# A hybrid decoder block on one core: gate, logit and projection jobs in a new order, one moving block for identity and router, residual added in a late expert

## The chip, the cores and the metric

One Trainium2 chip, one core of it. The metric is the device time of one launch in microseconds, the median of several runs. TensorE (PE in the profile) multiplies matrices into PSUM, its weight loads stand apart as PEld; VectorE is DVE, ScalarE is ACT, GpSimd is POOL. SyncE (SP) here issues transfers (DMA) and computes nothing. Each engine runs its own list of instructions in order and waits on semaphores.

## The reference

One layer with 256 tokens (T) of 1024 numbers, all in fp32: a mixer with two branches and then 32 experts.

```python
xn = rms_norm(x, norm1_g)
proj = xn @ w_in
u, q, k, v, qi, ki, wi, gs, ga = jnp.split(proj, IN_OFFSETS, axis=-1)
...
y_ssm = s5_mixer(u, ssm_parameters)         # diagonal complex scan over the tokens, gelu, GLU
y_att = dsa_attention(q, k, v, qi, ki, wi)  # indexer scores choose 64 keys a query, then softmax
mixed = g_ssm * (y_ssm @ w_proj_ssm) + g_att * (y_att @ w_proj_attn)
x = x + mixed @ w_out
x = x + moe(rms_norm(x, norm2_g), expert_weights)  # 4 of 32 experts a token, clamped SwiGLU
...
return rms_norm(x, norm_f_g)
```

The experts' weights are 32 times 12.6 MB and all are read.

## The kernel before

**Layout.** In the mixer features lie on the 128 partitions and tokens along the free axis. The weights of the mixer come as 27 chunks of 1 MB (CHUNKS) through four buffers (wbuf, NBUF = 4): SP loads a chunk once the job that used its buffer last is done. TensorE works them off as jobs (JOBS): a job (feature_job, L974) is 16 matmuls of 128 x 128 weights and 256 tokens into one of two PSUM banks (rot), which ScalarE or VectorE must empty before the job after next. The profile counts two instructions for each fp32 matmul, so 32 for a job. JOBS and CHUNKS fix positions that the semaphores count to, so the order in the lists and in each engine's program is written out by hand and must agree.

**Scan.** U0 and U1 give u. VectorE builds the table phase by doublings (doubled, 1 to 64), ScalarE (turned) and VectorE (finish_phase, L636) make its second half. In four rounds (round_) TensorE makes input products (bu, L1005), VectorE multiplies them by the phase, adds, scans (L689) and makes the output products (out_ok), and TensorE turns those into y (y_out, L1016). After round 3 the ropes rotate keys, indexer queries and queries, y_raw adds the skip (L728), ScalarE takes the gelu (L482) and GLU0 and GLU1 follow.

**Attention.** Score jobs (score_job, L1068) are laced into A0 and A1; ScalarE takes the relu, VectorE adds up 16 heads (scores, L744), chooses keys with MAX8 and MATCH_REPLACE8 (choose_keys), masks the logits (mask, L769 and L772; row_max), ScalarE takes exponentials (L470), VectorE divides (probabilities; prob_ok). TensorE turns them (L1097) and multiplies by v (attend, L1105). PS0 to PS3 project the scan's branch, L1138 the attention's; W0 to W7 (L1161) make the mixer's output, added to x1.

**Into the experts.** After each W job aux (L1149, L1150) turns the tile of x1 to token rows: a matmul against w_rout (router logits, 32 columns) and one against the identity (128 columns). The identity products stay in banks 4 to 7, where they serve three ends: the squares for the second norm (L502), the tokens' rows xs (L510), and as the residual, as all experts add into the same banks (scatter, L1203). VectorE then picks four experts a token (L816 to L837) and each expert's one-hot tile; TensorE gathers the rows (L1186), turns them (L1194), multiplies by the expert's input weights (L1227; biases L1238) and output weights (L1269).

**Transfers.** The experts' weights come in 12 parts of 2,097 KB for two experts at a time (load_first(n) loads part n; even experts use 0 to 5, odd 6 to 11). The first 12 go into room that the mixer has left, when it has left it; part 5 covers the room of gate_s. Later ones follow chunk_used, part by part.

## Time and profile before

| | |
|---|---|
| median of 3 runs | 1187.84 us (1187.19 to 1189.55) |
| profiled execution | 1187.95 us, its span 1186.1 us |
| mean granted clock of TensorE | 0.987 of 2.4 GHz |
| busy: PE, PEld, DVE, ACT, POOL | 1121.3, 493.6, 343.7, 152.6, 0.7 us |
| first expert matmul | 275.41 us from the start |
| moved by DMA | 436.49 MB, mean 368 GB/s |

The span runs from the first to the last instruction. All times in rows count from its start. A row of a timeline merges neighbouring instructions of one group: start, length, engine, line, what it writes and reads, how many, and in brackets how long the engine was idle before and who ended that. The busy share of an engine is an average over stages that have different limits; a stage has to be read by itself.

### The profile page before, as it was taken

How to read it: one execution, taken by the hardware profiler on the slowest of the kernel's cores; microseconds unless marked ns; L12 is line 12 of the kernel's file. 1: busy time of each engine (PE TensorE's matmuls, PEld its weight loads, DVE VectorE, ACT ScalarE, POOL GpSimd, SP SyncE). 2: the span in 40 equal slices, each digit the busy share in tenths (PEclk: the TensorE clock that was granted, in tenths of full speed). 3: DMA queues.
4: the chain of work that ended last, by engine and by line, in shares of the span. 5: the costliest groups of instructions: out<-in, count | busy, mean ns of one | idle time of the engine just before them, and what ended most of it. 6: DMA issues, size and time to landing. Idle time of an engine off the chain costs nothing.

```text
span 1186.1 us, 13814 instructions
## 1 busy us (share of the span) xinstructions
PE 1121.3 (95%) x5602; PEld 493.6 (42%) x5602; DVE 343.7 (29%) x745; ACT 152.6 (13%) x317; POOL 0.7 (0%) x7
## 2 busy tenths in 40 slices
PE   8989988988999999999999999999999999999995
PEld 6868776873333333333333333333333333333331
DVE  7999656312111111112221111111111111111112
ACT  2301234112001000001100100000000000000002
POOL 0000000000000000000000000000000000000000
PEclk9999998998999999999999999999999999999998
DMA  8224715857999999999999999999999999999993
GB/s 333 107 107 143 319 72 220 347 195 298 427 429 426 430 427 430 427 429 428 429 428 429 429 428 429 428 428 427 430 427 430 427 430 427 429 428 429 427 428 156
DMA packets 33290, 436.49 MB, mean 368 GB/s; under 512 B 3824, under 2 KB 4080, under 8 KB 5232
## 3 DMA queue, kind: packets, MB, share of 16 engines
q1 hardware_dynamic: 32976, 435.43, 87.5%
q10 hardware_dynamic: 288, 0.69, 0.2%
q8 instruction: 19, 0.31, 0.1%
q14 instruction: 7, 0.06, 0.0%
HBM read 435.06 MB, written 1.05 MB: 368 GB/s over the span
## 4 chain that ended last, share of the span: by engine, by line
PE 73%; DMA 13%; DVE 6%; SPq 4%; ACT 2%; issue 1%; another core or an unknown queue 0%; DVEq 0%
PE ps L1227 30%; PE ps L1269 15%; DMA mem<-in_w_moe 12%; PE ps L974 8%; PE ps L1186 4%; PE ps L1203 4%; DVE mem L559 4%; SPq L351 4%; PE ps L1161 2%; PE ps L1238 2%; PE ps L1194 1%; PE ps L1254 1%; PE ps L1138 1%; DVE mem L689 1%; PE ps L1068 1%
## 5 line engine op out<-in xcount | busy, mean ns | idle before, releaser
L1227 PE MATMUL ps<-mem,late 128*64 128x512 f32 x2048 | 458.2, 595 | 22.8 <-DMA mem<-in_w_moe 22.6
L1227 PEld LDWEIGHTS ps<-mem,late 128*64 128x64 f32 x2048 | 141.6, 137 | 330.7 <-issue 282.3
L1269 PE MATMUL ps<-mem,late 128*64 128x512 f32 x1024 | 226.8, 595 | 0.0
L902 DVE TENSOR_SCALAR late<-ps 128x512 f32<-128x512 f32 x32 | 22.1, 692 | 689.4 <-PE ps L1227 689.4
L974 PE MATMUL ps<-mem 128*128 128x256 f32 x640 | 148.3, 391 | 8.0 <-ACT mem L482 3.7
L974 PEld LDWEIGHTS ps<-mem 128*128 128x128 f32 x640 | 123.6, 196 | 31.0 <-issue 11.3
L1269 PEld LDWEIGHTS ps<-mem,late 128*64 128x64 f32 x1024 | 70.7, 137 | 133.3 <-issue 128.1
L522 ACT ACTIVATE late<-late 128x512 f32<-128x512 f32 x32 | 20.1, 630 | 514.8 <-DVE late L902 514.8
L1186 PE MATMUL ps<-xs,late 128*64 128x512 f32 x256 | 63.7, 619 | 1.1 <-ACT xs L510 1.1
L1203 PE MATMUL ps<-late 64*128 64x512 f32 x256 | 63.6, 615 | 0.8 <-ACT late L529 0.8
L559 DVE TENSOR_TENSOR mem<-mem 128x1024 f32<-128x1024 f32 (+7 forms) x83 | 60.5, 770 | 8.3 <-ACT mem L421 7.1
L529 ACT ACTIVATE late<-ps 128x512 f32<-128x512 f32 x32 | 19.1, 597 | 230.7 <-PE ps L1269 230.7
L559 DVE TENSOR_TENSOR late<-late 128x128 f32<-128x128 f32 (+2 forms) x98 | 38.4, 419 | 5.9 <-ACT late L513 0.3
L1203 PEld LDWEIGHTS ps<-late 64*128 64x128 f32 x256 | 22.1, 186 | 41.8 <-issue 41.8
L1238 PE MATMUL ps<-bias_rows,late 32*64 32x512 f32 x256 | 34.8, 613 | 0.0
L1186 PEld LDWEIGHTS ps<-xs,late 128*64 128x64 f32 x256 | 15.9, 138 | 43.4 <-issue 42.3
L559 DVE TENSOR_TENSOR late<-ps,vec 128x512 f32<-128x512 f32 x32 | 22.1, 692 | 38.8 <-PE ps L1194 38.8
L518 ACT ACTIVATE late<-ps 128x512 f32<-128x512 f32 x32 | 19.2, 599 | 76.9 <-PE ps L1186 76.9
L1161 PE MATMUL ps<-mem 128*128 128x256 f32 x128 | 28.8, 379 | 0.0
L559 DVE TENSOR_TENSOR mem<-ps,mem 128x1024 f32<-128x1024 f32 (+2 forms) x26 | 23.2, 932 | 11.3 <-PE ps L1138 11.1
L1161 PEld LDWEIGHTS ps<-mem 128*128 128x128 f32 x128 | 23.9, 190 | 3.0
L1254 PEld LDWEIGHTS ps<-table,late 128*128 128x128 f32 x128 | 13.4, 140 | 28.1 <-issue 24.3
(157 smaller groups left out, 515.2 us busy)
## 6 DMA issues: line engine op xcount, KB each, us to landing
mem<-in_w_moe SPq DMA_DIRECT2D x192, 2048.0 KB, 42.3
mem<-in_w_mix SPq DMA_DIRECT2D x27, 1024.0 KB, 5.8
out<-xs SPq DMA_DIRECT2D x2, 512.0 KB, 3.1
late<-in_mix_tables SPq DMA_DIRECT2D x1, 576.0 KB, 15.2
mem<-in_x_t ACTq DMA_DIRECT2D x1, 512.0 KB, 4.5
mem<-in_x_t SPq DMA_DIRECT2D x1, 512.0 KB, 5.8
mem<-in_b_blk SPq DMA_DIRECT2D x1, 512.0 KB, 10.5
mem<-in_c_blk SPq DMA_DIRECT2D x1, 512.0 KB, 16.0
```

The source lines that it names most:

```text
L351: sp.dma_start(place_of(half, n), expert_part(e, n)).then_inc(moe_in[half][n], 16)
L522: ac.activation(sig, gate_z, ACT.Sigmoid, scale=ALPHA).then_inc(sig_ok, 1)
L559: return ve.tensor_tensor(out_, a, b, op)
L902: ve.tensor_scalar(gate_z, z[:, 0], LIMIT, None, ALU.min).then_inc(z_gate, 1)
L974: i = pe.matmul(b[:, m * T:m * T + T], slot[:, k, (first_m + m) * P:(first_m + m + 1) * P], src[:, k, :], start=(k == 0), stop=(k == kt - 1))
L1161: i = pe.matmul(b[:, 0:T], wide(f"W{m // 2}")[:, k, (m % 2) * P:(m % 2) * P + P], mixed[:, k, :], start=(k == 0), stop=(k == KD - 1))
L1186: i = pe.matmul(ps[64 * q:64 * q + SLOTS, 3, :], one_hot[:, t, :], xs[:, t, 512 * q:512 * q + 512], start=(t == 0), stop=(t == TT - 1))
L1203: i = pe.matmul(ps[:, 4 + 2 * t + q, :], gated_t[r, t * P:t * P + P], y_tok[r, :], start=False, stop=False, skip_group_check=True)
L1227: i = pe.matmul(ps[r, n // 2, :], h_sel[:, k % 4, k // 4, :], w[:, 512 * n:512 * n + 512], start=(k == 0), stop=(k == KD - 1))
L1238: pe.matmul(ps[r, n // 2, :], chosen[g, n, :], b_in[g, :], start=False, stop=False)
L1254: i = pe.transpose(ps[:, 0, n * P:n * P + P], act[:, n * P:n * P + P], ident)
L1269: i = pe.matmul(ps[64 * q:64 * q + SLOTS, 2, :], act_tile(k), w[:, 512 * q:512 * q + 512], start=(k == 0), stop=(k == KF - 1))
```

## The change

It changes orders and a few operations, and the result is computed as before.

- U0's chunk is loaded in two halves, laid out so that the first half serves the first eight matmuls; the mean matmul goes between the halves. The square sums go ahead of the doublings, the doubling by 64 is split, and the first quarter releases ScalarE.
- finish_phase of the next round moves in front of the output products. The ropes of keys and indexer queries go ahead of round 3, that of the queries behind it with its own temporaries.
- TensorE's order: input and output products move a job later or earlier; score jobs are laced into S3 and A0; y_out(3) behind them; A1, A2 and logits(0) ahead of GLU; A3 and logits(1), PS0, PS1 between them and the turning of probabilities; attend(0) behind PS2 and PS3.
- scores takes the two token tiles in turn. VectorE evicts PS2 and PS3 itself and multiplies by the gate in two steps.
- aux is one matmul of 160 columns a tile against turn_w, identity and router columns side by side; its result is evicted (rpart, xs), the router's parts are added up by VectorE (rsum), x is scaled in place.
- The residual is added in the last expert but one by four matmuls with diag, the identity times the root, on the normed xs. The second expert's scatter opens the banks.
- Parts 5 and others are loaded at other points of SP's list. The title of the change also names GpSimd; its three memsets are not touched by the diff.

The diff, cut to its core:

```diff
...
-JOBS = ["U0", "U1", "KK", "QI0", "QI1", "QI2", "QI3", "VW", "Q0", "Q1", "S0", "S1", "S2", "S3", "KR0", "KR1", "KR2",
-        "A0", "A1", "GLU0", "GLU1", "A2", "A3", "P0_0", "P0_1", "PS0", "PS1", "PS2", "PS3"] \
+JOBS = ["U0", "U1", "KK", "QI0", "QI1", "QI2", "QI3", "VW", "Q0", "Q1", "S0", "S1", "S2", "KR0", "KR1", "KR2", "S3",
+        "A0", "A1", "A2", "GLU0", "GLU1", "A3", "PS0", "PS1", "P0_0", "P0_1", "PS2", "PS3"] \
...
-CHUNKS = ["U0", "U1", "KK", "QI0", "QI1", "QI2", "QI3", "VW", "Q0", "Q1", "S0", "S1", "S2", "S3", "A0", "A1", "GLU",
-          "A2", "A3", "PS0", "PS1", "PA0", "PA1", "W0", "W1", "W2", "W3"]
+CHUNKS = ["U0", "U1", "KK", "QI0", "QI1", "QI2", "QI3", "VW", "Q0", "Q1", "S0", "S1", "S2", "S3", "A0", "A1", "A2",
+          "GLU", "A3", "PS0", "PS1", "PA0", "PA1", "W0", "W1", "W2", "W3"]
...
-            load("U0")
+            sp.dma_start(wbuf[:, 0, 0:1024], io["w_mix"][0, :, 0:1024]).then_inc(u0_first, 16)
+            sp.dma_start(wbuf[:, 0, 1024:SW], io["w_mix"][0, :, 1024:SW]).then_inc(w_slot_in[0], 16)
...
-            sp.wait_ge(scanned, 4)
             sp.wait_ge(out_ok, 4)
             load_first(0, 1)
+            load("GLU")
             sp.wait_ge(y_raw_ok, 1)
             load_first(4)
-            for name in CHUNKS[CHUNK["A2"]:CHUNK["PA0"]]:
+            for name in CHUNKS[CHUNK["A3"]:CHUNK["PA0"]]:
                 load(name)
+            sp.wait_ge(row_max, 1)
+            sp.dma_start(turn_w, io["turn_w"].rearrange("p (k c) -> p k c", k=KD)).then_inc(rout_in, 16)
             sp.wait_ge(y_ssm_ok, 1)
             load_first(2)
+            load("PA0")
+            load("PA1")
             sp.wait_ge(row_max, 2)
             load_first(6)
-            for name in CHUNKS[CHUNK["PA0"]:CHUNK["W2"]]:
-                load(name)
-            sp.wait_ge(gate_s_used, 1)
-            load_first(5)
+            load("W0")
+            load("W1")
             sp.wait_ge(att_done, 2)
             load_first(7)
...
             sp.wait_ge(aux_done, KD)
             load_first(11)
+            sp.wait_ge(rstd_ok, 1)
+            load_first(5)
...
-                ac.wait_ge(half_ok, 1)
+                ac.wait_ge(half_ok, min(i, 1) + 1)
...
+            gate("S", gate_s, V_BG, 3)
+            ac.wait_ge(roped, 3)
+            relus(3, 4, 5, 6)
             gate("A", gate_a, V_BG + KD, 0)
-            ac.wait_ge(roped, 4)
-            relus(3, 4, 5, 6)
-            gate("A", gate_a, V_BG + KD, 1)
...
+            gate("A", gate_a, V_BG + KD, 1)
+            gate("A", gate_a, V_BG + KD, 2)
...
-            gate("A", gate_a, V_BG + KD, 2)
+            exponentials(0)
             gate("A", gate_a, V_BG + KD, 3)
-            exponentials(0)
+            for n in range(2):
+                evict(f"PS{n}", p_ssm[:, 2 * n:2 * n + 2, :], pair)
+            prob_turned(0)
+            exponentials(1)
             attended(0)
-            exponentials(1)
-            for n in range(4):
-                evict(f"PS{n}", p_ssm[:, 2 * n:2 * n + 2, :], pair)
+            prob_turned(1)
             attended(1)
...
+                b = ps[:, 2 + m % 2, 0:TT * (P + NE)].rearrange("p (t c) -> p t c", t=TT)
                 ac.wait_ge(aux_done, m + 1)
+                ac.activation(rpart[:, m], b[:, :, P:P + NE], ACT.Copy).then_inc(rpart_ok, 1)
...
+                    ac.activation(at(10 * SW + P * (TT * m + t), P), b[:, t, 0:P], ACT.Square,
+                                  accum_out=stat[:, 64 + KD * t + m:65 + KD * t + m]).then_inc(squared1, 1)
+                ac.activation(xs[:, :, m * P:m * P + P], b[:, :, 0:P], ACT.Copy).then_inc(tok_ok, 1)
...
-            ready(ACT.Exp)
+            ac.wait_ge(tok_ok, KD)
             ac.wait_ge(rstd_ok, 1)
             for t in range(TT):
-                for q in range(2):
-                    ac.activation(xs[:, t, 512 * q:512 * q + 512], ps[:, 4 + 2 * t + q, :], ACT.Copy,
-                                  scale=stat[:, 6 + t:7 + t]).then_inc(x_norm, 1)
+                ac.activation(xs[:, t, :], xs[:, t, :], ACT.Copy, scale=stat[:, 6 + t:7 + t]).then_inc(x_norm, 1)
+            ready(ACT.Exp)
...
             tt(squares[:, 0, :], squares[:, 0, :], squares[:, 1, :], ALU.add).then_inc(sq_sum, 1)
-            link(doubled(16))
+            link(doubled(1))
+            link(doubled(2))
+            link(doubled(4))
             ve.wait_ge(mean_done, 1)
             ve.tensor_scalar(squares[:, 0, :], ps[:, 2, 0:T], EPS, None, ALU.add).then_inc(var_ok, 1)
-            link(doubled(32))
+            link(doubled(8))
+            link(doubled(16))
...
             u_evict(0)
-            doubled(64).then_inc(half_ok, 1)
+            link(doubled(32))
+            doubled(64, 0, 4).then_inc(half_ok, 1)
             u_evict(1)
-            ve.wait_ge(half_ok, 1)
+            doubled(64, 4, NCH).then_inc(half_ok, 1)
...
-                finish_phase(i)
...
+                if i < 3:
+                    finish_phase(i + 1)
                 ve.wait_ge(scanned, i + 1)
                 if i:
                     ve.wait_ge(y_done, i)
...
+            ve.wait_ge(half_ok, 2)
+            finish_phase(0)
             round_(0)
             round_(1)
             round_(2)
-            round_(3)
             ve.wait_ge(consts_in, 16)
             rope(kk.unsqueeze(1), 1, "KK")
             rope(qi_t[:, 0:2], 2, "QI1")
             rope(qi_t[:, 2:4], 2, "QI3")
-            rope(q_t, 2, "Q1")
+            round_(3)
+            rope(q_t, 2, "Q1", temps=[at(4 * SW + 1024 * n, 2, 2, T) for n in range(2)])
...
+                        for t in range(TT):
+                            acc = score[:, t, 0:P * (t + 1)]
+                            s = relu[4 * t + hg][:, m, :]
+                            if m == 0:
+                                ve.wait_ge(score_free, 4 * t + hg + 1)
+                            if h == 0:
+                                ins = ve.tensor_scalar(acc, s, wi[:, t, h:h + 1], None, ALU.mult)
+                            else:
+                                ve.wait_ge(v_chain, behind[t])
+                                ins = ve.scalar_tensor_tensor(acc, s, wi[:, t, h:h + 1], acc, ALU.mult, ALU.add)
+                            ins.then_inc(v_chain, 1)
+                            chain[0] += 1
+                            behind[t] = chain[0]
...
-            choose_keys(1)
-            probabilities(0)
...
             tt(y_ssm, y_gelu, glu_g, ALU.mult).then_inc(y_ssm_ok, 1)
+            choose_keys(1)
+            probabilities(0)
+            ve.wait_ge(*evicted("PS1"))
+            ve.wait_ge(*evicted("PS0"))
+            tt(p_ssm[:, 0:4, :], p_ssm[:, 0:4, :], gate_s[:, 0:4, :], ALU.mult)
             mask(1)
...
+            tt(turn_w[:, :, P:P + NE], turn_w[:, :, P:P + NE],
+               vec[:, V_G2:V_G2 + KD].unsqueeze(2).to_broadcast([P, KD, NE]), ALU.mult).then_inc(w_gain, 1)
+            for n in (2, 3):
+                ve.wait_ge(rot_done, JOB[f"PS{n}"] + 1)
+                tt(p_ssm[:, 2 * n:2 * n + 2, :], bank_of(f"PS{n}").rearrange("p (k t) -> p k t", k=2),
+                   gate_s[:, 2 * n:2 * n + 2, :], ALU.mult).then_inc(*evict_mark(f"PS{n}"))
             probabilities(1)
...
+                if m:
+                    ve.wait_ge(rpart_ok, m)
+                    if m > 1:
+                        link(tt(rsum, rpart[:, 0] if m == 2 else rsum, rpart[:, m - 1], ALU.add))
...
+                for t in range(TT):
+                    ins = ve.tensor_scalar(diag[:, t, :], ident, stat[:, 4 + t:5 + t], None, ALU.mult)
+                ins.then_inc(diag_ok, 1)
...
             x_job("QI2")
+            x_job("QI3")
             y_out(0)
-            x_job("QI3")
-            bu(2)
             chunk_arrived(pe, "VW")
...
-            y_out(1)
+            bu(2)
             x_job("Q0")
             x_job("Q1")
+            y_out(1)
+            x_job("S0")
             bu(3)
-            x_job("S0")
+            x_job("S1")
             y_out(2)
-            x_job("S1")
             x_job("S2")
-            x_job("S3")
-            y_out(3)
...
-            x_job("A0", between=score_job)
-            x_job("A1", between=lambda step: score_job(4 + step))
...
+            x_job("S3", between=score_job)
+            x_job("A0", between=lambda step: score_job(4 + step))
+            y_out(3)
+            x_job("A1")
             pe.wait_ge(tables_in, 16)
+            x_job("A2")
+            logits(0)
             chunk_arrived(pe, "GLU")
...
-            x_job("A2")
-            logits(0)
             x_job("A3")
             logits(1)
+            pe.wait_ge(y_ssm_ok, 1)
+            ps_job(0)
+            ps_job(1)
+            turn_prob(0)
+            ps_job(2)
+            ps_job(3)
             attend(0)
-            pe.wait_ge(y_ssm_ok, 1)
-            for n in range(4):
-                if n % 2 == 0:
-                    chunk_arrived(pe, f"PS{n // 2}")
-                feature_job(f"PS{n}", y_ssm, KS, 2 * (n % 2), deep(f"PS{n // 2}"))
+            turn_prob(1)
             attend(1)
...
+                if m == 0:
+                    pe.wait_ge(w_gain, 1)
+                if m >= 2:
+                    pe.wait_ge(tok_ok, m - 1)
                 for t in range(TT):
-                    tile = x1[:, m, t * P:t * P + P]
-                    pe.matmul(ps[:, 2 + t, 0:NE], tile, w_rout[:, m, :], start=(m == 0), stop=(m == KD - 1))
-                    i = pe.matmul(ps[:, 4 + 2 * t + m // 4, (m % 4) * P:(m % 4) * P + P], tile, ident,
-                                  start=(m % 4 == 0), stop=False, skip_group_check=True)
+                    i = pe.matmul(ps[:, 2 + m % 2, t * (P + NE):(t + 1) * (P + NE)], x1[:, m, t * P:t * P + P],
+                                  turn_w[:, m, :], start=True, stop=True)
...
+                        scatter(j - 1, opens=opens)
+                        if adds:
+                            pe.wait_ge(diag_ok, 1)
+                            for t in range(TT):
+                                for q in range(2):
+                                    pe.matmul(ps[:, 4 + 2 * t + q, :], diag[:, t, :], xs[:, t, 512 * q:512 * q + 512],
+                                              start=False, stop=False, skip_group_check=True)
...
-                body(first + 1, pairs, 1)
+                body(first + 1, pairs, 1, opens=isinstance(c, int))
...
-                body(first + NE - 2, pairs + NE // 2 - 1, 0)
+                body(first + NE - 2, pairs + NE // 2 - 1, 0, adds=isinstance(c, int))
...
```

## Rows read from the trace of the kernel before

**Rows 1.** The page: GB/s moved in each of the 40 equal slices of the span.
```profile
GB/s 333 107 107 143 319 72 220 347 195 298 427 429 426 430 427 430 427 429 428 429 428 429 429 428 429 428 428 427 430 427 430 427 430 427 429 428 429 427 428 156
```

**Rows 2.** Windows: stretch; busy us (instructions) of each engine; PE clock, DMA share, GB/s.
```profile
400.00:500.00 100.00, 100.00 (x486) 33.99 (x486) 18.34 (x46) 8.97 (x15) 0.00 (x0) 1.00 1.01 429
```

**Rows 3.** Waits: engine, line, whom it waited for; us in total, times, longest.
```profile
PE ps L1227 <- DMA mem<-in_w_moe: 22.6, 25, 1.3
...
PE ps L1016 <- DVE mem L559: 5.2, 2, 2.7
```

**Rows 4.** Timeline of PE: start, us, what, xcount [idle before and its releaser].
```profile
1126.29 3.65 PE L1227 MATMUL ps<-mem,late 128*64 128x512 f32 x16 [1.26 <-DMA mem<-in_w_moe]
...
1129.87 1.99 PE L1203 MATMUL ps<-late 64*128 64x512 f32 x8
...
1131.79 1.94 PE L1186 MATMUL ps<-xs,late 128*64 128x512 f32 x8
```

**Rows 5.** Timeline of SP's queue from 0 to 300 us, its last issues.
```profile
280.43 18.85 SPq L351 DMA_DIRECT2D mem<-in_w_moe  x5
```

**Rows 6.** Windows in the mixer, columns as in rows 2.
```profile
26.00:61.00 35.00, 32.10 (x160) 26.66 (x160) 32.59 (x55) 11.71 (x36) 0.00 (x0) 0.95 0.35 125
...
183.00:208.00 25.00, 19.17 (x98) 16.17 (x93) 13.07 (x18) 11.37 (x39) 0.00 (x0) 0.86 0.70 270
```

**Rows 7.** Timeline of PE in the mixer, after its waits and undisturbed.
```profile
26.76 8.83 PE L974 MATMUL ps<-mem 128*128 128x256 f32 x32 [2.58 <-DVE mem L559]
...
157.56 15.74 PE L974 MATMUL ps<-mem 128*128 128x256 f32 x64 [3.71 <-ACT mem L482]
...
188.50 1.97 PE L1097 MATMUL ps<-table,xs 128*128 128x128 f32 x8 [5.05 <-DVE xs L559]
...
214.37 14.08 PE L1138 MATMUL ps<-mem 128*128 128x256 f32 x64 [0.69 <-ACT mem L478]
```

**Rows 8.** Timeline of PE and VectorE, start and rounds 0 to 3.
```profile
9.66 7.17 PE L974 MATMUL ps<-mem 128*128 128x256 f32 x32 [1.65 <-DMA mem<-in_w_mix]
...
36.06 2.19 DVE L636 SCALAR_TENSOR_TENSOR mem<-mem 128x128 f32<-128x128 f32 x8 [2.00 <-ACT mem L415]
...
56.58 4.63 DVE L559 TENSOR_TENSOR mem<-mem 128x1024 f32<-128x1024 f32 x4
...
100.57 4.62 DVE L559 TENSOR_TENSOR mem<-ps,mem 128x1024 f32<-128x1024 f32 x4
```

**Rows 9.** Timeline of PE from 150 to 216 us.
```profile
193.15 15.08 PE L974 MATMUL ps<-mem 128*128 128x256 f32 x64
```

**Rows 10.** Groups by form, then timeline: score additions and first step of key choice.
```profile
L744 DVE SCALAR_TENSOR_TENSOR mem<-late,mem 128x128 f32<-128x128 f32 x15 | 5.3, 352 | 3.8 <-ACT late L456 3.4
...
L744 DVE SCALAR_TENSOR_TENSOR mem<-mem 128x256 f32<-128x256 f32 x8 | 3.9, 485 | 2.1 <-ACT mem L456 1.9
...
176.94 0.42 DVE L559 TENSOR_TENSOR mem<-mem,late 128x256 f32<-128x256 f32 x1
```

**Rows 11.** Timeline of VectorE: the reduction behind tile 1's mask.
```profile
192.90 2.29 DVE L772 TENSOR_REDUCE stat<-xs 128x8 f32<-128x2048 f32 x1
```

**Rows 12.** Chain of work in order of time: start, us, what; two W jobs.
```profile
236.25 3.46 PE ps L1161 x16
...
240.59 3.46 PE ps L1161 x16
```

**Rows 13.** Timeline from the last aux to the first expert matmul.
```profile
263.14 0.38 PE L1149 MATMUL ps<-w_rout,mem 128*128 128x32 f32 x2 [0.81 <-ACT late L502]
...
268.92 0.29 DVE L559 TENSOR_TENSOR late<-table,late 128x128 f32<-128x128 f32 x1
...
269.60 3.68 PE L1186 MATMUL ps<-xs,late 128*64 128x512 f32 x8 [1.05 <-ACT xs L510]
...
275.41 1.94 PE L1227 MATMUL ps<-mem,late 128*64 128x512 f32 x8 [0.20 <-DVE late L559]
```

**Rows 14.** Timeline of ScalarE: a table load ahead of the exponentials.
```profile
182.40 1.28 ACT L470 ACT_TABLE_LOAD   x1
```

122 lines of the change are left out of this document (60 added, 62 removed).

## The prediction

> **What bounds the kernel now.** I read the 40 slices of the page first: from about 300 us on DMA moves 426 to 430 GB/s in every slice but the last [rows 1]. A table of windows says the same of one stretch of the expert loop, DMA share 1.01 and 429 GB/s [rows 2]. An expert is six parts of 2,097 KB; at 429 GB/s a part is 4.89 us and an expert 29.3 us. In the list of waits TensorE waits for such a part 25 times [rows 3]: it is faster than the transfers, eats the two experts that were loaded in advance, and then waits. The last such wait in order of time ends at 1126.29 us, in the last expert but one [rows 4]. So the end is this: the time at which the first used part can be loaded again, then 180 parts at the speed of the DMA, then a short tail. The first reload is issued at 280.43 us, 5.02 us after the first expert matmul at 275.41 us [rows 5]. What the mixer gives or takes ahead of 275.41 us moves the end one for one, as long as transfers are not the bound there, and they are not: DMA shares of 0.35 and 0.70 in long windows of the mixer [rows 6].
>
> Ahead of the experts TensorE is the bound in most stretches, with five waits of size: 2.58 us for the normed x, 2.5 and 2.65 us for the scan's output products (L1016, 5.2 together), 3.71 us for ScalarE's gelu, 5.05 us for the softmax [rows 3, 7]. It also pays for them in clock: windows around them show a mean granted clock of 0.86 and 0.95, a mixture of the levels of 1.2 and 2.4 GHz [rows 6]. The job after the first wait takes 8.83 us; undisturbed, two jobs' worth (64 instructions) take 14.08, so one takes 7.04 [rows 7].
>
> **The change, part by part.**
>
> *Start.* U0's weights come in two halves, so the first half no longer waits for 1 MB; U0 began at 9.66 us after a wait of 1.65 us for its load [rows 8]. I put it at 8.2. The mean matmul moves between U0's halves and the square sums move ahead of the doublings: 2.3 us of additions after 9.58 give sq_sum at about 12.0. U0 and U1 then end at about 23 (each job 7.0). VectorE keeps its work, but the wait of 2.00 us for ScalarE's turned tiles goes [rows 8], since the first quarter of the last doubling is released alone; splitting it adds four instructions, about 0.5 us. Round 0 started at 36.06 + 2.19 = 38.25 and now starts at 36.75 us. SP issues one transfer more at the start, about 0.5 us, and U1's weights, used from 16 us on, have that to spare. The key projection starts at about 23 in place of 26.76 and without its wait.
>
> *Rounds.* Round 0 now has the next finish_phase (2.19 us, as the row of 36.06) between scan and output products. Its output products started 56.58 - 38.25 = 18.33 us after it did [rows 8]; now 36.75 + 18.33 + 2.19 = 57.3, and they end 4.6 later, at 61.9. TensorE has done QI3 by then (23 + 7.1 for KK, 1.1 for the input products, four jobs, 1.1 again) and is idle from 60.5 to 61.9: a wait of 1.4 us for one of 2.50. TensorE's y_out(0) ends near 64.2, where it ended before, but QI3's 7.1 us lie behind it and not ahead. Rounds 1 and 2 keep their work: from the output products of round 0 to the start of round 3 it was 100.57 - 56.58 = 44.0 us [rows 8]; less a finish_phase of 2.2 that has moved ahead, out_ok(3) comes at about 99.1, ahead of TensorE, which reaches that step at 100.8. The ropes move ahead of round 3, as the score jobs need them before its output: roped(3) at 108.9, bu_used(4) at 113.5, TensorE's first score job at 114. None of this stops TensorE.
>
> *One long TensorE stretch.* From 64.28, the end of y_out(0), to 208.23, the end of the jobs that start at 193.15, is 143.9 us [rows 9]. Out of it come QI3 (7.1), the waits of 2.65, 3.71, 5.05 and 0.78 us, and what the low clock cost: 15.74 against 14.08 for 64 matmul instructions (1.7), 15.08 against 14.08 (1.0), 1.97 for eight transposes that take 1.2 at the full clock (0.8), the first of two attends (1.0), 0.6 in QI3. What remains is about 120 us of work, and the same work stands in the new order between 64.2 and the end of attend(0): 184.5 to 185.5, if no new wait comes. I check the new order for that. y_out(3) stands behind the score jobs, at 135 to 136.9, so VectorE waits there from 129 to 136.9 with y_raw behind it and all scores behind y_raw. y_raw ends at 138.6 and gelu (table load and 1.06 us) at about 141, while TensorE is busy with A1, A2 and logits(0) until 152.1: the wait of 3.71 us goes. Scores: the two token tiles alternate, so the chained instructions no longer wait for one another. 32 instructions of 352 and 485 ns [rows 10], less some 70 ns of overlap, are 11.3 us (13.4 if nothing overlaps): 150 to 152. Key choice of tile 0 is 6.9 us, its mask 2.5: row_max(1) at about 159.3 to 161.5, ahead of logits(1) on TensorE at 166. y_ssm at 161.3; PS0 starts at 168. Key choice of tile 1 began at 176.94, and at 188.45 the product behind it ended, on which TensorE waited [rows 7, 10]; less that product (1.2), a reciprocal (0.2) and a wait in front of it (0.6) the choice is 9.4 us. Then probabilities(0): 172.2, ahead of turn_prob(0) at 175. So the wait of 5.05 us goes as well.
>
> *What is late next.* VectorE now waits for PS1's eviction (175.8), multiplies (1.2), and only then masks tile 1: 2.29 us and a reduction of 2.29 [rows 11]: 181.7. Exponentials 8 x 0.50, reciprocal and product 2.5: prob_ok(2) at 188.3. TensorE has ended attend(0) at 185.5 and waits 2.8 us. From the end of PS3 to L1138 it was 214.37 - 208.23 = 6.1 us [rows 7, 9]; I add 1.3 for the clock after the wait: L1138 at 195.7. It was 214.37. Gain 18.6 us.
>
> *Loads.* What SP's queue moves still lands in time, at 4.9 us a part: GLU, behind two expert parts issued at 125, lands near 140 and is used at 152. turn_w (655 KB in place of 128 KB) is released by row_max(1) and used 50 us later. Part 5 moves to rstd_ok. So parts 10, 11 and 5 are issued within the last 12 us before the first expert matmul: 14.7 us of transfer from the end of W7, against 16.8 us until the first reload. It just fits; part 5 is needed only at the end of expert 0.
>
> *W and aux.* A period was 240.59 - 236.25 = 4.34 us, of which 3.46 is W [rows 12]. The rest, 0.88, is aux: per token tile a matmul of 32 and one of 128 moving columns, now one of 160. The 128-column ones take about 0.15 us an instruction and there are four, so with a little for 32 more columns 0.66. Six periods give 1.3 us. The last aux waited 0.81 us for the squares of the one before [rows 13]; with alternating banks it does not: with its own 0.2 and the wait, 1.5. ScalarE now has 1.6 us of work an aux, under the period of 4.1.
>
> *Router.* Behind the last aux come one more eviction (0.25) and one more addition (0.2): 0.4 later. x no longer waits for the exp table load: that took x_norm to 269.5. But the one-hot tile was ready at 269.2 only (0.29 us from 268.92), so the gather at 269.60 gains 0.35 at most [rows 13], which I leave out. The sum for this stage is 2.8 - 0.4 = 2.4 us. The first expert matmul comes 18.6 + 2.4 = 21.0 us earlier, at 254.4.
>
> *The residual.* Four matmuls of 128 rows and 512 columns in the last expert but one. A job of 16 matmuls of 256 columns is 7.1, so 512 columns are 0.88: 3.5 us; with a change of tile shape 3.6. They stand where TensorE has no wait left: the last wait is that at 1126.29, and from L1203 on TensorE runs through [rows 4]. Bounds: 1.9 (L1203's four, which share the array by two) and 7.0 (all at the lower clock). I take 3.6. The Trainium skill, TensorEngine Tiling (Array Packing), Key Properties, has it that a change of tiling mode drains TensorE, which speaks against this edit, as it puts a 128-row shape between a 64-row and a 64-column one. The trace agrees in kind: the four of L1203 take 1.92 us from start to start, 0.2 over two times 0.86 [rows 4]; with such a drain on both sides the edit would be 3.9 and the end 0.3 later.
>
> *Tables.* ScalarE's order now needs sigmoid, exp, sigmoid, exp in attention: two more loads. The row of the trace has 1.28 us for one, with the next instruction right behind it [rows 14]; both lie ahead of waits (for A3's matmuls and for row_max(2)), so I charge nothing, and up to 2.6 us if that cover is gone. The Trainium skill, ScalarE: Activation LUTs, What ACT_TABLE_LOAD costs, adds a drain of about 1.38 us to each load; by it the uncovered case is 5.3 us, the end 1175.7. The row does not show that drain.
>
> *GpSimd.* The diff leaves the three memsets of GpSimd as they are; nothing is counted.
>
> **Sum.** -21.0 + 3.6 = -17.4 us. The profiled execution took 1187.95 us with a span of 1186.1; the 1.85 us around the span stay. It becomes a span of 1168.7 and a time of 1170.55, and as the median of the runs is 0.11 below it, 1187.84 - 17.4 = 1170.4 us.
>
> **Rivals.**
> (a) VectorE becomes the bound of attention. The wait for y_out(3) puts everything on VectorE behind 136.9. If scores don't overlap (2.1), if the table loads come uncovered (2.6) and if the added waits of TensorE bring the lower clock again (1.7 each), the gain shrinks by 4 to 8: 1174.5 to 1178.5, say 1176.5. For it: VectorE's idle 7.8 us and the wait of 2.8 are already in my walk. Against: TensorE has 7 us of slack at GLU.
> (b) More than I count: the residual costs 1.9, the gather (3.68 us, against 1.94 for the same in the loop [rows 4, 13]) runs at the full clock, and the wait before tile 1 is short: 1.7 + 1.7 + 2 = 5.4 better, 1165.0. Against: parts 10, 11 and 5 fill the DMA until then, which caps it.
> (c) Slower. The clock: the stretch of many 32-row score matmuls, 22 us of work, and the jobs after it run at the lower level. Each us of work at 1.2 GHz costs one more; from 17.4 us on the change loses; at 25 us the time is 1170.4 + 25 = 1195. For it: clocks of 0.86 and 0.95 in stretches with waits [rows 6]. Against: a stretch in which TensorE never rests shows 1.00 [rows 2], and the new order has fewer rests.
> (d) The change does not do what it says for the end: the parts loaded last hold the reloads where they are, and only residual and saved mixer cancel. If the first reload stays within 3.6 us of its place, 1187.8 +- 2. Against: the shares of DMA in the mixer [rows 6].
>
> **How the numbers follow.** Forecast 0.60 (1166.5 to 1174.5), (a) 0.22, (b) 0.11, (c) 0.04, (d) 0.03. Range 1163 to 1180. What a measurement can tell from no change is about 0.2%, 2.4 us. Faster is the forecast, (a) and (b) and some of (c): 0.94; same 0.02; slower 0.04.
>
> **What would show it.** First reload (L351) at 259 to 260 us; round 0 at 36.8; no wait of TensorE over 1 us between 64 and 180 us; one of 2 to 4 before turn_prob(1); L1138 at 195 to 196.5; aux period 4.1; gather right behind the one-hot tile; four matmuls of 3.6 us behind L1203 in the last expert but one; DMA at 429 GB/s without a gap after it starts. The prediction is wrong if VectorE's scores end after 153 us, if DMA has a gap or a queue at the first reload, or if the clock stays low beyond single jobs.

## The result and the profile after

| | before | changed |
|---|---|---|
| time, median of the runs (lowest to highest) | 1188.66 us (1187.19 to 1189.55) | 1170.00 us (1168.51 to 1171.77) |
| ratio, 95% interval | | 0.9845 (0.9826 to 0.9864) |
| profiled execution, span | 1187.95 us, 1186.1 us | 1169.42 us, 1167.6 us |
| mean granted clock of TensorE | 0.987 | 0.992 |
| first reload issued | 280.43 us | 258.72 us |
| last wait for a part ends | 1126.29 us | 1104.68 us |

The change takes 18.5 us off the span; the forecast was 17.4. The page's line of GB/s in 40 equal slices of the changed kernel answers rows 1, the windows answer rows 2 and 6 (stretch; busy us and instructions of PE, PEld, DVE, ACT, POOL; PE clock, DMA share, GB/s):

```profile
GB/s 334 145 145 109 266 261 216 217 321 430 427 427 428 430 428 428 429 428 428 429 429 428 428 430 429 427 429 429 428 428 429 429 427 429 429 429 427 428 429 105
```
```profile
26.00:61.00 35.00, 34.43 (x180) 29.02 (x178) 34.45 (x67) 12.35 (x37) 0.00 (x0) 1.00 0.37 138
61.00:81.00 20.00, 18.91 (x135) 16.28 (x136) 19.90 (x28) 1.14 (x4) 0.00 (x0) 1.00 0.46 158
183.00:208.00 25.00, 19.87 (x117) 17.14 (x118) 8.12 (x15) 7.01 (x18) 0.00 (x0) 0.80 0.72 281
400.00:500.00 100.00, 100.00 (x484) 33.87 (x482) 19.99 (x48) 9.61 (x16) 0.00 (x0) 1.00 1.01 428
```

The DMA is full one slice earlier (slice 10 holds 430 GB/s where it held 427 from slice 11 on), at the same speed. TensorE's clock in 26 to 61 us is 1.00 in place of 0.95; in 183 to 208 us it is 0.80, lower than the 0.86 of before [rows 6], though the two kernels do different work in those 25 us.

The list of TensorE's waits in the changed kernel (engine, line, whom it waited for; us in total, times, longest) answers rows 3:

```profile
PE ps L1277 <- DMA mem<-in_w_moe: 22.7, 25, 1.2
PE ps L1136 <- DVE xs L574: 3.7, 1, 3.7
PE ps L1219 <- DVE late L865: 3.6, 1, 3.6
...
PE ps L1056 <- DVE mem L574: 1.7, 1, 1.7
```

The waits for parts are the same 25 and the same sum. Of the five waits of the mixer two are left: 1.65 us for the scan's first output products and 3.67 us for tile 1's probabilities. The router's 3.6 us stand behind W and aux.

TensorE's timeline of the changed kernel (start, us, line, output and inputs, shape, count, in brackets the idle time before and its releaser), from the start to the tail; it answers rows 4, 7 to 9, 12 and 13 (between two rows marked with dots, rows are left out):

```profile
8.63 3.72 PE L1010 MATMUL ps<-mem 128*128 128x256 f32 x16
...
187.68 3.77 PE L1136 MATMUL ps<-table,xs 128*128 128x128 f32 x16 [3.67 <-DVE xs L574]
192.23 3.71 PE L1147 MATMUL ps<-mem 128*64 128x128 f32 x32 [0.78 <-ACT mem L429]
...
225.44 0.71 PE L1200 MATMUL ps<-late,mem 128*128 128x160 f32 x4
...
229.44 0.71 PE L1200 MATMUL ps<-late,mem 128*128 128x160 f32 x4
...
248.07 3.51 PE L1236 MATMUL ps<-xs,late 128*64 128x512 f32 x8 [0.81 <-DVE late L574]
...
1104.68 3.65 PE L1277 MATMUL ps<-mem,late 128*64 128x512 f32 x16 [1.25 <-DMA mem<-in_w_moe]
1108.26 1.99 PE L1253 MATMUL ps<-late 64*128 64x512 f32 x8
1110.18 3.70 PE L1303 MATMUL ps<-xs,diag 128*128 128x512 f32 x8
1113.81 1.94 PE L1236 MATMUL ps<-xs,late 128*64 128x512 f32 x8
```

Between the aux of one W job and the next lie 4.00 us (225.44 to 229.44), where it was 4.34. The residual takes 3.63 us from start to start (1110.18 to 1113.81) and stands behind the last wait for a part. SP's queue and VectorE, same columns:

```profile
258.72 10.62 SPq L359 DMA_DIRECT2D mem<-in_w_moe  x4
```
```profile
36.79 4.62 DVE L574 TENSOR_TENSOR mem<-ps,mem 128x1024 f32<-128x1024 f32 x4
...
57.31 4.63 DVE L574 TENSOR_TENSOR mem<-mem 128x1024 f32<-128x1024 f32 x4
...
175.24 1.23 DVE L574 TENSOR_TENSOR mem<-mem 128x1024 f32<-128x1024 f32 x1 [3.65 <-ACT mem L429]
176.38 2.28 DVE L791 SCALAR_TENSOR_TENSOR xs<-ps,mem 128x2048 f32<-128x2048 f32 x1
```

The first reload is 21.7 us earlier, and so is the end of the last wait, 21.6 us. The sum of the span is then: -21.6 of mixer and router, +3.63 of residual, and -0.5 at the very end (the last matmul's wait for its own issue is 2.28 us here and was 2.74). ScalarE's timeline, the gelu and the first exponentials: the table load for gelu (at 135.65) lies ahead of a wait, the one for the exponentials does not:

```profile
138.23 1.06 ACT L492 ACTIVATE mem<-mem 128x1024 f32<-128x1024 f32 x1 [1.30 <-DVE mem L745]
...
158.66 0.84 ACT L498 ACTIVATE mem<-ps,vec 128x256 f32<-128x256 f32 x2 [2.61 <-PE ps L1010]
159.52 1.28 ACT L478 ACT_TABLE_LOAD   x1
160.81 0.40 ACT L478 ACTIVATE xs<-xs,stat 128x128 f32<-128x128 f32 x1
```

The last term of the sum is not the change's: the same wait is 2.3 to 2.8 us in the kernels below, without an order in it.

### The profile page after: what moved, and what is told of

The parts are those of the page before. It is cut to its first block, busy times and chain, and to the rows that moved or that the text cites. A ratio compares the mean times of both kernels' runs of the same rounds, so it can differ in the third digit from the quotient of the medians.

```text
span 1167.6 us, 13800 instructions
## 1 busy us (share of the span) xinstructions
PE 1118.3 (96%) x5578; PEld 490.3 (42%) x5578; DVE 343.2 (29%) x760; ACT 157.2 (13%) x331; POOL 0.7 (0%) x7
## 4 chain that ended last, share of the span: by engine, by line
PE 63%; DMA 22%; SPq 7%; DVE 6%; issue 1%; ACT 1%; DVEq 0%
PE ps L1277 25%; DMA mem<-in_w_moe 21%; PE ps L1325 13%; PE ps L1010 7%; SPq L359 7%; PE ps L1236 4%; PE ps L1253 3%; DVE mem L574 3%; PE ps L1211 2%; PE ps L1288 2%; PE ps L1188 1%; PE ps L1244 1%; PE ps L1310 1%; PE ps L1056 1%; PE ps L1107 1%
## 5 line engine op out<-in xcount | busy, mean ns | idle before, releaser
L1277 PE MATMUL ps<-mem,late 128*64 128x512 f32 x2048 | 458.2, 595 | 22.9 <-DMA mem<-in_w_moe 22.7
L1010 PE MATMUL ps<-mem 128*128 128x256 f32 x640 | 143.4, 382 | 0.0
L1010 PEld LDWEIGHTS ps<-mem 128*128 128x128 f32 x640 | 119.9, 190 | 21.0 <-issue 4.5
L1236 PE MATMUL ps<-xs,late 128*64 128x512 f32 x256 | 63.5, 618 | 0.8 <-DVE late L574 0.8
L574 DVE TENSOR_TENSOR mem<-mem 128x1024 f32<-128x1024 f32 (+8 forms) x89 | 61.2, 729 | 6.5 <-ACT mem L429 3.7
L1211 PE MATMUL ps<-mem 128*128 128x256 f32 x128 | 28.8, 379 | 0.0
L1211 PEld LDWEIGHTS ps<-mem 128*128 128x128 f32 x128 | 24.0, 190 | 3.0
L1310 PEld LDWEIGHTS ps<-table,late 128*128 128x128 f32 x128 | 13.4, 140 | 28.1 <-issue 24.3
```

The lines of the kernel that those rows point to most:

```text
L574: return ve.tensor_tensor(out_, a, b, op)
L1010: i = pe.matmul(b[:, m * T:m * T + T], slot[:, k, first_m + m, :], src[:, k, :], start=(k == 0), stop=(k == kt - 1))
L1211: i = pe.matmul(b[:, 0:T], wide(f"W{m // 2}")[:, k, m % 2, :], mixed[:, k, :], start=(k == 0), stop=(k == KD - 1))
L1236: i = pe.matmul(ps[64 * q:64 * q + SLOTS, 3, :], one_hot[:, t, :], xs[:, t, 512 * q:512 * q + 512], start=(t == 0), stop=(t == TT - 1))
L1277: i = pe.matmul(ps[r, n // 2, :], h_sel[:, k % 4, k // 4, :], w[:, 512 * n:512 * n + 512], start=(k == 0), stop=(k == KD - 1))
L1310: i = pe.transpose(ps[:, 0, n * P:n * P + P], act[:, n * P:n * P + P], ident)
```

## The experiments

Each experiment is one edit of the changed kernel; where an order is changed, the lists and the other engines follow it. Two theories run through them. The first: the end is the first reload plus a constant, so every microsecond of TensorE's path ahead of the experts counts whole, and behind the last wait for a part every microsecond of TensorE counts whole. The second: that slack (in the loads, in VectorE's idle time) takes in part of what is added or removed. This table, from the timelines of all profiled executions, is the common test; the tail is the span less the time at which the last wait for a part ends.

| kernel | first reload, us | last wait ends, us | between, us | tail, us | median, us | ratio to before (95%) |
|---|---|---|---|---|---|---|
| before | 280.43 | 1126.29 | 845.9 | 59.8 | 1188.66 | |
| changed | 258.72 | 1104.68 | 846.0 | 62.9 | 1170.00 | 0.9845 (0.9826 to 0.9864) |
| a0_after | 258.39 | 1104.20 | 845.8 | 63.0 | 1169.78 | 0.9845 (0.9831 to 0.9858) |
| e1_no_residual | 259.94 | 1105.85 | 845.9 | 59.5 | 1167.17 | 0.9828 (0.9812 to 0.9844) |
| e2_residual_early | 262.91 | 1109.14 | 846.2 | 59.4 | 1167.94 | 0.9821 (0.9808 to 0.9835) |
| e3_scores_chained | 258.37 | 1104.53 | 846.2 | 63.5 | 1171.23 | 0.9836 (0.9818 to 0.9854) |
| e4_start_old | 263.20 | 1109.12 | 845.9 | 63.5 | 1174.93 | 0.9888 (0.9869 to 0.9908) |
| e5_y0_first | 268.96 | 1114.80 | 845.8 | 63.0 | 1180.13 | 0.9924 (0.9906 to 0.9942) |
| e6_warm_attention | 257.89 | 1103.73 | 845.8 | 63.3 | 1168.69 | 0.9822 (0.9804 to 0.9841) |
| e7_warm_router | 258.26 | 1104.81 | 846.6 | 63.4 | 1168.72 | 0.9828 (0.9810 to 0.9847) |
| e8_turn_first | 253.50 | 1099.31 | 845.8 | 63.4 | 1164.85 | 0.9803 (0.9790 to 0.9816) |
| e9_aux_split | 261.70 | 1107.71 | 846.0 | 63.0 | 1171.58 | 0.9844 (0.9827 to 0.9861) |
| e10_aux_one_bank | 261.90 | 1107.79 | 845.9 | 63.0 | 1173.72 | 0.9857 (0.9837 to 0.9877) |
| e11_all | 253.48 | 1100.36 | 846.9 | 59.3 | 1160.87 | 0.9750 (0.9733 to 0.9767) |

Over first reloads 27 us apart (253.5 to 280.4) the time from the first reload to the last wait is 845.8 to 846.2 us, but for the two kernels with dummy matmuls in the router, to which I come. Medians of the kernel before moved by 1.5 us from one comparison to the next, so for single terms below the rows decide. No run puts the old order of jobs in attention back: that the waits of 3.71 and 5.05 us went with it is read from the two timelines and not tested by itself.

**The changed kernel again.**

> The changed kernel itself, to have it beside the experiments on the same chip. 1170 us, and in its profile the first reload at 258.7 us, the last wait of TensorE for a part at 1104.7 us and the residual's four matmuls at 1110.2 us.

It came within 0.5 us of each of these: first reload 258.39, last wait 1104.20, residual at 1109.70; the median is 1169.78.

**Without the residual.**

```diff
-                body(first + NE - 2, ..., 0, adds=isinstance(c, int))
+                body(first + NE - 2, ..., 0, adds=False)
```

> Leaves the residual out (the four matmuls with the diagonal tile); the output lacks it. Theory: they stand behind TensorE's last wait for a part, so their whole 3.63 us lie on the path that sets the end: 3.6 us less than the changed kernel, about 1166.4, with the first reload where it was. Rival 1: TensorE has slack there after all, then 0. Rival 2: the change of tile shape costs a drain on both sides, then 3.9 less.

The kernel leaves the residual out, so its output is not the layer's. The median fell by 2.6 us beside the changed kernel on the same chip, the tail by 3.5 (63.0 to 59.5); the intervals of the two ratios overlap, so the rows carry this reading. TensorE's timeline without the residual:

```profile
112.35 3.61 PE L1010 MATMUL ps<-mem 128*128 128x256 f32 x8
```
```profile
1109.44 1.99 PE L1253 MATMUL ps<-late 64*128 64x512 f32 x8
1111.36 1.94 PE L1236 MATMUL ps<-xs,late 128*64 128x512 f32 x8
```

The gather stands 1.92 us behind the scatter's start, where the changed kernel has 5.55 (1108.26 to 1113.81): the difference is 3.63, four matmuls of 0.88 and 0.1 over. The slack rival falls, and so does the one with a drain on both sides. The first row shows why the profiled execution gained 1.9 only and not 3.5: the eight matmuls behind the KR jobs ran at the lower clock, 3.61 us in place of 1.97, ahead of any code that differs. The first reload came 1.55 us later than on the same chip in the changed kernel.

**The residual in the second expert.**

```diff
-                body(first + 1, pairs, 1, opens=isinstance(c, int))
+                body(first + 1, pairs, 1, opens=isinstance(c, int), adds=isinstance(c, int))
```

> The same four matmuls behind the first scatter, in the second expert, where TensorE still has loaded experts in hand and waits for parts later. Theory: its waits for parts shrink by 3.6 us in sum (22.7 to about 19.1) and the end comes 3.6 us earlier than in the changed kernel, about 1166.4, as if the residual were not there. Rival: the delay passes on through the release of the second expert's parts to the reloads, then no gain (1170).

The tail is 59.4 us, as if the residual were not there, and the waits for parts shrank from 22.7 to 19.9 us, 2.8 for an expected 3.6:

```profile
PE ps L1277 <- DMA mem<-in_w_moe: 19.9, 21, 1.2
```
```profile
196.73 16.04 PE L1188 MATMUL ps<-mem 128*128 128x256 f32 x64 [0.69 <-ACT mem L488]
```

So the four matmuls fill time in which TensorE would have waited for parts, and the rival (the delay passes on to the reloads) falls: from the first reload to the last wait it is 846.2 us, 0.2 to 0.4 more than in the two profiles of the changed kernel. The median is 1.8 us under the changed kernel (intervals of the ratios 0.9808 to 0.9835 and 0.9831 to 0.9858), and the profiled execution even has its first reload at 262.91. Again it is the clock, ahead of the edit: the projections behind attend(1) took 16.04 us in place of 14.08, and more in the router (window 242 to 262: 0.74 in place of 0.91). The best of its runs, 1165.52 us with a mean clock of 0.993, is 3.5 us under the best of the changed kernel on the same chip (1169.06 at 0.992) and 3.0 under the best of all its runs (1168.51 at 0.993). So the residual costs 3.6 us where it stands and at most 0.4 in the second expert; the rows show this, the medians alone would not.

**Probabilities of tile 0 turned earlier.**

```diff
-            ps_job(1)
             turn_prob(0)
+            ps_job(1)
...
+            mask(1)
             tt(p_ssm[:, 0:4, :], p_ssm[:, 0:4, :], gate_s[:, 0:4, :], ALU.mult)
-            mask(1)
...
             for n in (2, 3):
+                if n == 3:
+                    probabilities(1)
```

> TensorE turns the first tile's probabilities after PS0 in place of after PS1, VectorE masks tile 1 ahead of the two products on p_ssm and takes the last of them behind the probabilities of tile 1, ScalarE evicts in the order of the jobs. Theory: the wait of 3.67 us ahead of tile 1's transposes came from VectorE's order alone (mask waits behind PS1's eviction and a product). Worked out from the trace: the mask starts at 173.1 in place of 176.4, prob_ok(2) comes at 184.4 in place of 187.7, the wait is 0.4 us. The clock then stays at its full level: transposes of tile 1 take 2.4 in place of 3.8, attend(1) 2.0 in place of 3.7. The first projection on the attention output starts 6 us earlier (190.6 in place of 196.6) and all behind it with it: 1164. Rival: VectorE's work is the bound and another wait takes the place of this one: the gain is 1.5 us or less, 1168.5 to 1170. Second rival: the wait goes but the low clock comes all the same: 3.3 us, 1166.7.

Left out of the diff: JOBS and ScalarE's evictions in the same order. VectorE's and TensorE's timeline of this kernel:

```profile
172.83 2.29 DVE L791 SCALAR_TENSOR_TENSOR xs<-ps,mem 128x2048 f32<-128x2048 f32 x1 [1.26 <-PE ps L1137]
```
```profile
185.29 2.60 PE L1137 MATMUL ps<-table,xs 128*128 128x128 f32 x16 [0.67 <-DVE xs L574]
188.68 1.99 PE L1148 MATMUL ps<-mem 128*64 128x128 f32 x32 [0.78 <-ACT mem L429]
191.35 14.08 PE L1189 MATMUL ps<-mem 128*128 128x256 f32 x64 [0.69 <-ACT mem L488]
```

The mask starts 3.5 us earlier, the wait of 3.67 us is 0.67, and transposes and attend(1) run at the full clock (1.00 from 183 to 208 us): projections at 191.35 in place of 196.62, 5.3 us earlier for an expected 6. The median is 1164.85, for an expected 1164. The wait that was left in the changed kernel came from the order of VectorE's work, not from its amount.

**The old start.** Left out of the diff: doublings 1, 2, 4 and 8 stand ahead of the square sums, and the last doubling is undivided.

```diff
-            sp.dma_start(wbuf[:, 0, 0:1024], ...).then_inc(u0_first, 16)
-            sp.dma_start(wbuf[:, 0, 1024:SW], ...).then_inc(w_slot_in[0], 16)
+            load("U0")
...
-            feature_job("U0", ..., between=mean_between)
+            feature_job("U0", ...)
+            pe.matmul(ps[:, 2, 0:T], ones, squares[:, 0, :], start=True, stop=True).then_inc(mean_done, 1)
```

> The start of the kernel before in the changed kernel: first weights in one transfer, doublings ahead of the square sums, the mean's matmul behind the first job, the last doubling undivided. Theory: the start was worth 1.5 us because the scan's round 0 decides when the first output products are there: round 0 at 38.25 in place of 36.8, TensorE's wait ahead of them 1.5 us longer, the first reload 1.5 us later, 1171.5. Rival: TensorE itself is the bound there (it loses the 2.58 us at the key projection again), 2.5 us or more, 1172.5. Second rival: the start has slack, 0.

Median 1174.93, by the ratios 5.1 us over the changed kernel: my theory fell, and the first rival was right in kind but too small. TensorE's timeline:

```profile
26.64 8.83 PE L1008 MATMUL ps<-mem 128*128 128x256 f32 x32 [2.70 <-DVE mem L573]
...
65.58 1.93 PE L1057 MATMUL ps<-mem 128*32 128x256 f32 x32
```

The key projection waits 2.70 us again (2.58 before the change) and runs at the lower clock, 8.83 us as there [rows 7]. The first output matmuls are then reached by TensorE at 65.58 with no wait at all, 3.5 us behind their place in the changed kernel (62.09): TensorE and not the scan is late. The first reload is 4.5 us later in this execution (263.20): 3.5 from the start, 1.6 from the eight matmuls behind the KR jobs, which took 3.62 us at the lower clock, less 0.6 in attention and router. That stretch at the lower clock shows with the new start too, so only the 3.5 us are surely the start's.

**The scan's first output matmuls ahead of QI3.**

```diff
+            y_out(0)
             x_job("QI3")
-            y_out(0)
```

> The scan's first output matmuls back ahead of QI3, all else as changed. Theory: they can't start before 62.1 us, so TensorE stands idle from 53.3 us on and QI3's 7.1 us come behind: everything behind is 7.1 us later, the first reload at 265.8, and the time is 1177, with up to 1.5 more by the clock after an idle time of nearly 9 us. This is the test of one for one: what the mixer loses ahead of the experts the end loses. Rival: slack later in the mixer (VectorE's idle 8.1 us, TensorE's wait of 3.67) takes in some of it, 1173 to 1175.

The first reload is 10.2 to 10.6 us later, the median 1180.13 (by the ratio 9.4 us over the changed kernel). TensorE's timeline:

```profile
62.04 3.64 PE L1056 MATMUL ps<-mem 128*32 128x256 f32 x32 [8.56 <-DVE mem L574]
65.61 7.83 PE L1010 MATMUL ps<-mem 128*128 128x256 f32 x32
```

QI3's 7.1 us are as expected; the output matmuls after the 8.56 us of idle time take 3.64 us in place of 1.93 and QI3 0.7 more than its 7.17. With 1.6 us more behind the KR jobs in this execution, and 0.6 less in attention, that makes up the 10.4 us. TensorE's later wait of 3.67 us is still there, and VectorE's idle time ahead of L745, 8.1 us in the changed kernel, grew to 18.7 us, as its list of waits says:

```profile
DVE mem L745 <- PE ps L1056: 18.7, 1, 18.7
```

So the slack rival falls: a wait whose releaser is TensorE takes in nothing of what TensorE is late.

**Dummy matmuls in attention's wait.**

```diff
             attend(0)
+            keep_busy(8, 3)
             turn_prob(1)
```

> Eight dummy matmuls (3.5 us) into the free bank between attend(0) and the transposes of tile 1, where TensorE waits 3.67 us; nothing else. Theory: the low clock behind the wait (0.80 from 183 to 208, 3.77 for 16 transposes and 3.71 for attend(1) against 2.4 and 2.0 at the full clock) is caused by the idle time; with TensorE busy it goes, and all behind is 2.8 us earlier: 1167.2, clock 0.97 or more from 183 to 208. Rival: the low clock is caused by the shape of that work, not by the idle time before it: no change, 1170.

Windows (columns as above) and TensorE's timeline:

```profile
183.00:208.00 25.00, 23.27 (x147) 19.87 (x148) 9.40 (x18) 6.78 (x17) 0.00 (x0) 1.00 0.72 285
242.00:262.00 20.00, 16.89 (x68) 6.92 (x70) 5.17 (x26) 5.80 (x7) 0.00 (x0) 0.74 0.81 328
```
```profile
187.67 1.10 PE L1136 MATMUL ps<-table,xs 128*128 128x128 f32 x8
...
193.61 6.74 PE L1189 MATMUL ps<-mem 128*128 128x256 f32 x30 [0.69 <-ACT mem L488]
```

Transposes start at the same 187.67, but the projections start at 193.61 in place of 196.62: 3.0 us, for an expected 2.8. The clock of the window went from 0.80 to 1.00. So the idle time and not the shape of the work brings the lower clock there. In this execution most of it was given back in the router and the first expert's start, whose clock was 0.74 (0.91 in the changed kernel): the first reload, at 257.89, is only 0.8 us earlier. By the ratios the kernel gains 2.7 us.

**Dummy matmuls in the router.**

```diff
             aux(KD - 1)
+            dummies(8)
             pe.wait_ge(picked_ok, 1)
...
+            dummies(2)
```

> Eight dummy matmuls after the last aux and two after the rank matmuls, in the idle times of 3.6 and 0.8 us ahead of the gather. Theory: the gather runs at the full clock, 1.9 us in place of 3.5, the first expert matmul starts at 252.0 in place of 253.7 and the first reload is issued at 257.0. Parts 10, 11 and 5 keep the DMA busy up to 258, and from there it idled for over 2 us until the reloads flowed, so the gain comes through whole: 1168.4. Rival: those three parts hold the reloads where they are, 1170, or let only the 0.7 us between 258.0 and 258.7 through, 1169.3.

Windows of the changed kernel, then of this one:

```profile
258.00:259.00 1.00, 1.00 (x8) 0.36 (x6) 0.00 (x0) 0.00 (x0) 0.00 (x0) 1.00 0.05 16
259.00:260.00 1.00, 1.00 (x6) 0.29 (x4) 0.00 (x0) 0.00 (x0) 0.00 (x0) 1.00 1.24 229
260.00:261.00 1.00, 1.00 (x8) 0.35 (x6) 0.00 (x0) 0.00 (x0) 0.00 (x0) 1.00 0.29 66
```
```profile
258.00:259.00 1.00, 1.00 (x8) 0.34 (x6) 0.00 (x0) 0.00 (x0) 0.00 (x0) 1.00 0.84 360
259.00:260.00 1.00, 1.00 (x6) 0.29 (x4) 0.00 (x0) 0.00 (x0) 0.00 (x0) 1.00 0.93 213
260.00:261.00 1.00, 1.00 (x8) 0.38 (x6) 0.00 (x0) 0.00 (x0) 0.00 (x0) 1.00 0.61 213
```

```profile
249.18 1.94 PE L1242 MATMUL ps<-xs,late 128*64 128x512 f32 x8
```

The gather takes 1.94 us in place of 3.51. More than a third of it is lost again: from the first reload to the last wait it is 846.6 us in place of 846.0. In the changed kernel the transfers of parts 10, 11 and 5 are over by 258 us, ahead of the first reload (258.72), and DMA rests until that one flows (16, 229, 66 GB/s). Here they still run when the first reload is issued (258.26; 360, 213, 213 GB/s). They also started later: in this execution the eight matmuls behind the KR jobs took 3.61 us, and the last aux ended at 244.04 in place of 242.99. By the rows the gain is 1.6 us less 0.6, between theory and rival (0.7 us let through); by the ratio it is 2.0. The runs do not tell the two apart, only that the parts loaded last take in some of the gain.

**Scores chained again.**

```diff
-                for hg in range(4):
-                    for m in range(4):
-                        for t in range(TT):
+                for t in range(TT):
+                    for hg in range(4):
+                        for m in range(4):
```

> The scores of the two token tiles one after the other in place of alternating, so that each chained instruction waits for the one before. VectorE's scores take longer: 10.4 us now, 12.5 to 13.4 then. Theory: no time, 1170, because VectorE waits 3.65 us for PS1's eviction behind them, which takes in the 2 to 3 us; turn_prob(0) at 174.4 still finds its probabilities (they would come at 173.7 to 174.6), and the last wait of tile 1 stays at 187.7. Rival: VectorE bounds attention, and the time grows by the 2 to 3 us, 1172 to 1173.

VectorE's timeline of this kernel:

```profile
148.38 4.20 DVE L763 SCALAR_TENSOR_TENSOR mem<-mem 128x256 f32<-128x256 f32 x8
...
175.13 1.23 DVE L574 TENSOR_TENSOR mem<-mem 128x1024 f32<-128x1024 f32 x1 [1.19 <-ACT mem L429]
```

The scores end at 152.6 in place of 148.5, so alternating saves 4.1 us, more than the 2 to 3 I expected. None of it arrives: the same product starts at 175.1, behind a wait that is 1.19 us where it was 3.65, and TensorE's wait before tile 1 is 3.67 us as before, the first reload at 258.37. The median (1171.23; ratio 0.9836, the interval overlaps that of the changed kernel) shows no difference that I would build on, and the rows show none.

**Aux in two matmuls; aux in one bank.**

```diff
-                    i = pe.matmul(ps[..., t * (P + NE):(t + 1) * (P + NE)], x1[...], turn_w[:, m, :], ...)
+                    pe.matmul(ps[..., t * (P + NE) + P:(t + 1) * (P + NE)], x1[...], turn_w[:, m, P:], ...)
+                    i = pe.matmul(ps[..., t * (P + NE):t * (P + NE) + P], x1[...], turn_w[:, m, 0:P], ...)
```

> Identity and router columns in two matmuls (128 and 32 columns) in place of one of 160, banks and all else as changed. Theory: TensorE bounds the output projection, so the period grows from 4.00 to about 4.2 us, in eight of them 1.6 us: first reload 1.6 later, 1171.4. Rival: the columns decide, not the count of instructions: 4.00, 1170. Second rival: each extra matmul costs its weights anew, 4.34 as before, 1172.5.

The other kernel also has bank 2 where the changed one has 2 + m % 2:

```diff
-                if m >= 2:
-                    pe.wait_ge(tok_ok, m - 1)
+                if m >= 1:
+                    pe.wait_ge(tok_ok, m)
...
```

> Aux results in one bank in place of two in turn. Theory: in the periods nothing changes, as ScalarE has done with an aux (1.6 us) before the next (3.4 us later); only the last aux stands right behind the one before and waits for ScalarE, 1.3 to 1.5 us, all of it on the path: first reload 1.4 later, 1171.2. Rival: ScalarE is late anyway and what it does behind the last aux decides: 0.

TensorE's timeline, first with the aux in two, then with one bank:

```profile
221.81 0.30 PE L1200 MATMUL ps<-late,mem 128*128 128x32 f32 x2
...
226.16 0.30 PE L1200 MATMUL ps<-late,mem 128*128 128x32 f32 x2
```
```profile
243.33 0.78 PE L1200 MATMUL ps<-late,mem 128*128 128x160 f32 x4 [1.20 <-ACT xs L519]
```

In two matmuls the period is 4.35 us, the 4.34 of before the change, so the second rival holds: the last aux ends 2.5 us later than in the changed kernel. With one bank the periods stay at 4.00, the last aux waits 1.20 us and ends 1.1 us later. Each kernel's first reload is later by more (3.0 and 3.2 us) as the router behind it ran at a lower clock (gather at 250.97 and 249.56, clock 0.83 and 0.74 from 242 to 262 us). Their medians are 1.6 and 3.7 us over 1170.00, their ratios 0.9844 and 0.9857, so the timing alone does not tell the first from no change; the rows do.

**Together.** Attention as in the turn-first kernel, the residual in the second expert, dummies in the router.

> The reordered attention of the turn-first kernel, the residual in the second expert, and the dummy matmuls ahead of the gather, together. Theory: from the turn-first kernel's 1164.9 come off 3.6 us in the tail (residual, by the two runs without it there) and 0.6 to 1.3 by the gather at the full clock; 0.6 if the DMA is the bound at the first reloads, as it was in the run with dummies alone, where the last wait came 0.7 us later behind the first reload than elsewhere. 1160.5. Rival: the gains don't add, because the parts loaded last now hold all of the reloads: 1162 or more.

1160.87 us for an expected 1160.5, ratio 0.9750 (0.9733 to 0.9767) to before: 9 us under the changed kernel by the medians, 11 by the ratios, and the fastest here. Timelines of TensorE and of SP's queue:

```profile
244.40 1.94 PE L1243 MATMUL ps<-xs,late 128*64 128x512 f32 x8
```
```profile
253.48 30.33 SPq L359 DMA_DIRECT2D mem<-in_w_moe  x8
```

The tail is 59.3 us. The first reload is where the turn-first kernel has it (253.48 and 253.50): the dummies' gain is used up in this execution by the eight matmuls behind the KR jobs (3.12 us). From the first reload to the last wait it is 846.9 us, 1.0 over the others, so most of the dummies' gain at the gather is lost to the parts loaded last. From the end of the last aux to the first reload it is 14.2 us in both kernels with dummies and 15.7 in the changed one; the three parts that are released from W7's end on are 14.7 us of transfer (three times 4.89). So I read that under about 15 us the mixer's end no longer sets the stream, the loads do; no run loads these parts earlier to test it.

## Why the prediction was right, point by point

The mechanism was right: the mixer gained, and the end followed one for one. The sum came closer than its terms. Up to the start of L1138 the change gained 17.75 us for a forecast of 18.6, from there to the first expert matmul 3.95 for a forecast of 2.4, and the end gave 0.5 that the forecast did not have. That the first two errors have opposite signs is luck. First reload (258.72) and L1138 (196.62) lie just outside the places I had named (259 to 260, 195 to 196.5).

- **The bound, and one for one.** Right. The table above has it over 27 us of first reloads. What moved the first reload moved the end. The 180 parts of the forecast are not what lies in between: 845.9 us at 4.89 each are about 173 parts (an estimate), and the last seven land while TensorE no longer waits, which is why its work counts whole there. I had called a gap in DMA at the first reload a sign of being wrong. There is one (16, 229 and 66 GB/s from 258 to 261 us), but it was a bad sign to set: in the kernel before DMA rests for 7 us ahead of the first reload's transfer (274 to 281 us), and the time from the first reload to the last wait is the same.
- **Start.** Round 0 at 36.79 (forecast 36.75), U0 at 8.63 (8.2), no wait ahead of the key projection. The old start put back shows that this part was worth more than a reader of the scan alone would say: 3.5 us of TensorE's path in rows, and 5 in time, where some of the rest is a stretch at the lower clock.
- **Rounds.** Output products at 57.31 (57.3), TensorE's wait 1.65 us (1.4), no other wait up to 187 us that belongs to the scan.
- **One long stretch.** attend(0) ended at 184.0, half a microsecond ahead of the range (184.5 to 185.5), scores at 148.5 (150 to 152), row_max(1) at 158.0 (159.3 to 161.5). The waits of 3.71 and 5.05 us are gone. The scores term was mis-sized: 10.4 us for a forecast of 11.3, and 14.6 if chained, where I had 13.4 at most. It cost nothing, as VectorE waits behind them anyway.
- **What is late next.** The place was right: VectorE's mask behind PS1's eviction. prob_ok(2) at 187.6 (188.3), the wait 3.67 us (2.8). The term for the clock behind it was mis-sized: 1.3 us taken, 3.0 measured by the dummies that removed it. L1188 at 196.62 (195.7). That I counted this wait among the slack that a change leaves, and not as the next thing to remove, was the dear omission: turning the probabilities one job earlier gives 5 us on top of the change.
- **Loads.** Right: the list of waits has none for a chunk of the mixer's weights. It was closer than forecast at the end: parts 10, 11 and 5 flowed until 258.0 us, 0.7 ahead of the first reload, where I had 2.1 to spare.
- **W and aux.** Forecast 2.8 us, measured 3.5: from the projections to the first expert matmul it is 57.1 us in place of 61.0, of which 0.25 is router and 0.2 the gather itself. The period fell by 0.34 and not by 0.22, as I had 0.66 us for the two blocks of an aux and they take 0.55; split again, the period went back to 4.35. For the last aux I had 1.5, but the two terms that I named for it, 0.2 and the wait of 0.81, make 1.0; with one bank it waits 1.20 and ends 1.1 later.
- **Router.** Forecast 0.4 later, measured 0.2 earlier (5.08 from the end of the last aux to the gather; 5.32 before). The gather is released by the one-hot tile, as forecast, and runs at the lower clock (3.51 us).
- **Residual.** 3.6, measured 3.63, all on the path. By the Trainium skill, TensorEngine Tiling (Array Packing), Key Properties, a change of tiling mode drains TensorE; with 0.2 us on both sides I had 3.9 by it. The rows show 0.1 over four times 0.88 in all, so here the drain costs nothing that would change a decision.
- **Tables.** Right: the loads cost the end nothing. ScalarE still waited 1.30 us between the one for gelu and y_raw, and it waited 0.27 and 3.17 us behind the two that the new order adds. The load ahead of tile 0's exponentials stands uncovered, and ScalarE goes from the end of one activation (159.50) to the start of the next (160.81) in 1.31 us. The drain of about 1.38 us that the Trainium skill (ScalarE: Activation LUTs, What ACT_TABLE_LOAD costs) adds to a load does not show there; the measurement decides, and an uncovered load costs 1.3 us here.
- **Rivals.** (a) VectorE as the bound: in the end it did bound one point, tile 1's mask, by its order. (b) More gain: none of its three parts came by itself, and the cap by parts 10, 11 and 5 that I put against it is what the dummies ran into. (c) A slow clock at the start of the 32-row stretch did show, in five of the thirteen profiles of changed kernels and for 1.1 to 1.6 us. (d) fell with the first reload.

## What to carry to other kernels

- Where a stream of transfers sets the end, find the event that starts the stream and measure each edit there: "first reload plus 845.9 us plus tail" told more than the medians, which move by 1 to 2 us with the clock. Work that stands behind the last wait of the stream costs whole; the same work earlier, where the engine still waits for the stream, costs nothing.
- A wait that is left after a reordering has two prices, itself and the lower clock behind it (3.67 and 3.0 us here). Ask what stands ahead of the releaser on its engine: moving one mask past one product and one transposition past one job was worth 5 us.

## What the runs showed of the hardware that I had not expected

- The same instructions ran at different clocks in different executions: the eight matmuls behind the KR jobs took 1.97 us in eight profiles (both of the changed kernel, e2, e3, e6, e8, e9, e10), 3.58 to 3.62 in four (e1, e4, e5, e7) and 3.12 in one (e11), with nothing different ahead of them in e1 and e7. One such drop is up to 1.6 us, more than several of the terms here. What decides whether it comes is open.
- A table load of ScalarE with nothing to wait for on either side took 1.31 us from the end of one activation to the start of the next (159.50 to 160.81).
- Chained additions of 256 columns started 0.53 us apart (4.20 us for eight); a chained pair of 128 and 256 columns took 0.91 us (14.6 us for sixteen), an alternating pair 0.66, less than the sum of the two durations that the profile gives (0.34 and 0.48).
- From start to start a matmul of 32 moving columns took 0.14 us and one of 128 took 0.31 us in the kernel with two, and the block of 160 took 0.27 us (an aux of two blocks from 225.44 to 225.99): the 32 columns more cost nothing that the rows show, a matmul of their own cost 0.17 us a token tile (periods of 4.35 and 4.00 us). Why the block of 160 is no slower than one of 128 is open.
